# A two-block transformer kernel: weight split moved behind convolution and token sums on VectorE, and three projections back to eight block products

## The chip, the cores and the metric

The kernel runs on one core of one Trainium2 chip. The metric is the device time of one execution in microseconds; lower is better. The kernel before takes 2741.47 us (median of three runs, 2741.23 to 2741.66).

The engines are named as in the profile: PE is TensorE (PEld its weight loads), DVE is VectorE, ACT is ScalarE, POOL is GpSimd, SP is SyncE, which here issues the weight loads. All of them run their own instruction stream in order and wait for one another through semaphores.

## The reference

Two transformer blocks run one after the other on 512 tokens of width 1024, all in float32. Between them they hold five feed-forward networks (FFNs) with a hidden width of 2816, which take most of the time. The first has a short convolution on its gate, the other four are SwiGLU layers:

```
def conv_ffn(n, w_up, conv_w, conv_b, w_down):          # FFN 0
    u, g = jnp.split(n @ w_up, 2, axis=-1)
    gp = jnp.pad(g, ((0, 0), (pad, pad), (0, 0)))
    gc = sum(gp[:, j:j + S] * conv_w[j] for j in range(CONV_WIDTH)) + conv_b
    return (jax.nn.silu(gc) * u) @ w_down

def swiglu(x, w_gate, w_up, w_down):                    # FFNs 1 to 4
    return (jax.nn.silu(x @ w_gate) * (x @ w_up)) @ w_down
```

Each FFN reads an RMS-normalised input and adds its result to the residual stream. Around them stand a linear recurrence, windowed attention, cross attention to a memory, a pooling and latent-attention mixer and a gated convolution mixer. The change does not touch those.

## The kernel before, in words

**Numbers as pairs.** Every float32 operand of a product is held as two parts: `hi`, the value rounded to the type that TensorE multiplies, and `lo`, the rest. A product is three matmuls (lines 2023 to 2025): hi by hi, lo by hi, hi by lo. Weights arrive in chunks of 128 x 2048 values. SP loads a chunk into one of two `stage` buffers, ACT writes `w_hi` (line 525), DVE writes `w_lo = stage - w_hi` (line 1024, `split_lo`, called by `ffn_lo`), and PE waits for `w_lo` (semaphore `lo_ready`) before it begins the chunk. All three buffers exist twice, so the split of chunk p+2 can begin only when PE has finished chunk p.

**The order of an FFN.** `ORDER` lists the 30 chunks of an FFN: `gate 0, up 0, gate 1, up 1`, then `gate it, up it, down it-2` for `it` from 2 to 9, then `gate 10, up 10`. Four short chunks follow (the "tail", the last part of the down projection). I call a place in this list p: chunk 0 is gate 0, chunk 2 gate 1, chunk 4 gate 2, chunk 5 up 2, chunk 6 down 0, chunk 7 gate 3. A gate or an up chunk gives two tiles of 128 hidden columns by 512 tokens.

**Eight or seven products.** A gate or up chunk is a product of 2 x 2 blocks. The plain form (`eight`) does it with 48 matmuls of 512 columns. The other form (`seven_products`) is a Strassen scheme: seven block products, 84 matmuls of 256 columns. Which chunk takes which form is in the table `SEVENS`. The seven-product form needs sums of token blocks (`token_sums`, lines 1090 to 1095, once per FFN, rounded into `t_hi` by ACT and `t_lo` by DVE at line 1100), sums of weight blocks for every chunk (`weight_sums`, lines 1050 to 1055, four instructions, and `s_hi`, `s_lo` by line 1037), and five instructions instead of one to collect the result from PSUM (`evacuated`, lines 1075 to 1083). In FFN 0 the gates 3 to 10 and the ups 4, 6 and 8 use seven products, the other chunks eight. In FFNs 1 to 4 gates and ups use seven from `it` = 2 on.

**The order on DVE.** DVE does one step per chunk p, begun when PE has finished chunk p (line 1154): it evacuates the result from PSUM, makes the weight sums of chunk p+2 if that is a seven-product up, splits the weights of chunk p+2 (`ffn_lo`), then does in FFN 0 the convolution of a gate (`convolved`, six instructions, lines 1145 to 1149), then the token sums that are due at this p (`T_SUMS`: in FFN 0 half of them at p = 0 and half at p = 2, in the other FFNs all at p = 0), then `t_lo`, the weight sums of a gate at p+3, and `f_lo`, the lo part of the finished hidden tiles. At the start of an FFN a statistic over the tokens (line 2063 or 2068 on PE, a square root on ACT, a reciprocal on DVE, line 1104) has to be there before the first evacuation.

ACT applies the SiLU to the gate (line 603 in FFN 0, 606 in the others), POOL multiplies gate and up (line 1901), ACT rounds the product to `f_hi` (line 615), and down chunks read `f_hi` and `f_lo`.

Of the kernel before, what the change touches and what calls it, by code (L numbers as in the profile page):

```python
# [51 lines left out]
STEPS = FT // 2  # L52
# [13 lines left out]
TILES = {"gate": 2, "up": 2, "down": 4}  # L66
TILE_AT = [sum(TILES[kind] for kind, _ in ORDER[:p]) for p in range(len(ORDER) + 1)]
LAST_K = 4 * ((STEPS - 3) // 2)
SEVENS = [{"gate": range(3, STEPS), "up": range(4, STEPS - 1, 2)}] + 4 * [{"gate": range(2, STEPS), "up": range(2, STEPS - 1)}]


def _ffn(i):
# [59 lines left out]
def past(n):  # L132

    return n + 1


def free(ap, offset, dims):

    return bass.AP(tensor=ap.tensor, offset=ap.offset + offset, ap=[ap.ap[0]] + dims)


def build(nc, stream, x_in, mem_in, pos_in, par_in, const_in, out):
    ctx = ExitStack()
    with ctx:
# [154 lines left out]
        def sem(name):  # L299
            return ctx.enter_context(nc.semaphore(name))  # L300
# [24 lines left out]
        f_hi_ready, f_ready = sem("f_hi_ready"), sem("f_ready")  # L325
# [64 lines left out]
        SINGLES = 3 * KP * P  # L390
        SEVEN_ORDER = [(i, p) for i in range(5) for p, (kind, it) in enumerate(ORDER) if kind != "down" and it in SEVENS[i][kind]]
        NTH = {at: n for n, at in enumerate(SEVEN_ORDER)}
# [13 lines left out]
        def two_banks(p):  # L406

            return 6 if p % 2 == 0 else 0

        def four_banks(p):  # L410

            return 4 * (p % 2 == 0)
# [10 lines left out]
        T_SUMS = [{0: [0, 1], 2: [2, 3]}] + 4 * [{0: [0, 1, 2, 3]}]  # L423
# [588 lines left out]
        def _(dve):  # L1012
# [48 lines left out]
            def evacuated(i, p, to):  # L1061

                if (i, p) not in NTH:
                    b = two_banks(p)
                    dve.tensor_tensor(to, ps[:, b:b + 2, :], free(rstd[:, :], 0, [[0, 2], [1, S]]), ALU.mult).then_inc(acc_evac, 2)
                    return
                n, bank = NTH[i, p], four_banks(p)

                def product(which, dims):
                    b, half = PRODUCT[which]  # L1070
                    return free(ps[:, bank + b, :], HALF * half, dims)

                adjacent, twice_dims = [[HALF, 2], [1, HALF]], [[0, 2], [1, HALF]]
                dve.wait_ge(first_copied, n + 1)
                dve.tensor_tensor(blocks[:, 0:2, :], product(2, adjacent), free(first, 0, twice_dims), ALU.add).then_inc(blocks_sum, 1)
                dve.wait_ge(blocks_sum, 4 * n + 1)
                dve.tensor_tensor(blocks[:, 2, :], product(7, [[1, HALF]]), blocks[:, 1, :], ALU.add).then_inc(blocks_sum, 1)
                dve.wait_ge(blocks_sum, 4 * n + 2)
                dve.tensor_tensor(free(blocks[:, 1, :], 0, [[S, 2], [1, HALF]]), product(5, twice_dims), blocks[:, 1:3, :], ALU.add).then_inc(blocks_sum, 1)
                dve.wait_ge(blocks_sum, 4 * n + 3)  # L1080
                dve.tensor_tensor(blocks[:, 1:3, :], product(3, adjacent), blocks[:, 1:3, :], ALU.add).then_inc(blocks_sum, 1)
                dve.wait_ge(blocks_sum, 4 * n + 4)
                dve.tensor_tensor(to, free(blocks[:, 0, :], 0, [[S, 2], [1, S]]), free(rstd[:, :], 0, [[0, 2], [1, S]]), ALU.mult).then_inc(acc_evac, 2)  # L1083

            def token_sums(i, j):

                done, gain = 16 * i + 4 * j, (pc(GAIN[i], j), pc(GAIN[i], KP + j))
                b12, b21, b22 = h[:, j, HALF:S], h[:, KP + j, 0:HALF], h[:, KP + j, HALF:S]
                dve.wait_ge(t_scaled, 4 * i + j + 1)
                dve.scalar_tensor_tensor(t_f[:, T1, j, :], b12, gain[0], t_f[:, T3, j, :], ALU.mult, ALU.subtract).then_inc(t_sum, 1)  # L1090
                dve.wait_ge(t_sum, done + 1)
                dve.scalar_tensor_tensor(t_f[:, T2, j, :], b22, gain[1], t_f[:, T1, j, :], ALU.mult, ALU.subtract).then_inc(t_sum, 1)
                dve.wait_ge(t_sum, done + 2)
                dve.tensor_tensor(t_f[:, T3, j, :], t_f[:, T2, j, :], t_f[:, T3, j, :], ALU.subtract).then_inc(t_sum, 1)
                dve.scalar_tensor_tensor(t_f[:, T4, j, :], b21, gain[1], t_f[:, T2, j, :], ALU.mult, ALU.subtract).then_inc(t_sum, 1)
# [38 lines left out]
            def ffn(i):  # L1134

                scale = SCALE[f"down{i}"]

                def convolved(it):

                    for e in range(2):  # L1140
                        f = 2 * it + e
                        g = gate_b[:, e, :]
                        if e == 0:
                            dve.wait_ge(acc_evac, T0["up0"] + TILE_AT[ORDER.index(("gate", it))] + 2)
                        dve.tensor_scalar(up_b[:, e, :], g[:, 1:1 + S], pc("conv_w1", f), pc("conv_b", f), ALU.mult, ALU.add).then_inc(conv_step, 1)
                        dve.wait_ge(conv_step, 6 * it + 3 * e + 1)
                        dve.scalar_tensor_tensor(up_b[:, e, :], g[:, 0:S], pc("conv_w0", f), up_b[:, e, :], ALU.mult, ALU.add).then_inc(conv_step, 1)
                        dve.wait_ge(conv_step, 6 * it + 3 * e + 2)
                        dve.scalar_tensor_tensor(up_b[:, e, :], g[:, 2:2 + S], pc("conv_w2", f), up_b[:, e, :], ALU.mult, ALU.add).then_inc(conv_step, 1)

                for p, (kind, it) in enumerate(ORDER):
                    c, t = chunk_at(i, p)
                    f, k = FT * i + 2 * it, 2 * it % 8
                    dve.wait_ge(chunk_done, c + 1)
                    if kind == "down":
                        b, m = four_banks(p), 4 * (it % 2)
                        if i == 1 and it < 2:
                            dve.wait_ge(renormed, KT + m + 4)
                        dve.scalar_tensor_tensor(h[:, m:m + 4, :], ps[:, b:b + 4, :], scale, h[:, m:m + 4, :], ALU.mult, ALU.add).then_inc(acc_evac, 4)
                    elif kind == "gate":  # L1160
                        evacuated(i, p, gate_b[:, :, 1:1 + S])
                    elif it < STEPS - 1:
                        dve.wait_ge(f_ready, past(f))
                        if i == 0:
                            dve.wait_ge(silu_ready, f + 2)
                        evacuated(i, p, up_b[:, :, :])
                    else:
                        dve.wait_ge(f_ready, past(f))
                        for e in range(2):
                            if i == 0:  # L1170
                                dve.wait_ge(silu_ready, f + 2)
                            dve.tensor_tensor(up_b[:, e, :], ps[:, two_banks(p) + e, :], rstd[:, :], ALU.mult).then_inc(acc_evac, 1)
                        for e in range(2):
                            dve.wait_ge(f_hi_ready, f + e + 1)
                            dve.tensor_tensor(f_lo[:, k + e, :], up_b[:, e, :], f_hi[:, k + e, :].bitcast(F32), ALU.subtract).then_inc(f_ready, 1)
                    if kind_at(i, p + 2) == ("up", True):
                        weight_sums(i, p + 2)
                    ffn_lo(i, p + 2)
                    if kind == "gate" and i == 0:
                        dve.wait_ge(f_ready, past(f))  # L1180
                        convolved(it)
                    for j in T_SUMS[i].get(p, []):
                        token_sums(i, j)
                    if p == T_ROUND[i]:
                        token_lo(i, 0)
                        token_lo(i, 1)
                    if p == T_ROUND[i] + 1:
                        token_lo(i, 2)
                        token_lo(i, 3)
                    if kind_at(i, p + 3) == ("gate", True):  # L1190
                        weight_sums(i, p + 3)
                    if kind == "up" and it < STEPS - 1:
                        dve.wait_ge(f_hi_ready, f + 2)
                        dve.tensor_tensor(f_lo[:, k:k + 2, :], up_b[:, :, :], f_hi[:, k:k + 2, :].bitcast(F32), ALU.subtract).then_inc(f_ready, 2)
                    if i == 1 and (kind, it) == ("gate", 1):
                        dve.wait_ge(std_ready, NS0["renorm"] + 1)
                        dve.reciprocal(sq[:, :], ssum[:, :]).then_inc(rstd_ready, 1)
# [335 lines left out]
            for i, (j, side) in enumerate(BRANCHES):  # L1533
                gate = gates(j)
# [1371 lines left out]
```

## Time and profile before

| | |
|---|---|
| median of three runs | 2741.47 us |
| the profiled execution | 2741.47 us, of which its span is 2739.7 us |
| PE busy | 2708.2 us, 99% of the span |
| DVE busy | 2120.1 us, 77% |
| ACT busy | 1012.1 us, 37% |
| POOL busy | 594.2 us, 22% |
| TensorE clock granted, mean | 0.999 of full speed |
| DMA | 97 GB/s in the mean |

The span is the time from the first to the last instruction of the profiled execution, and 1.8 us lie around it. "Busy" counts the time in which an engine executes. Matmuls overlap in the pipeline, so the start of one to the start of the next says more than the duration of one. A row of the trace gives the start in us from the span's start, the duration in us, the engine, the line, the operation, the names written and read, the shape, and in square brackets how long the engine sat idle before it and what released it. `w_hi`, `w_lo` and `stage` stand without their buffer number.

### The profile page before, as it was taken

How to read it: one execution, taken by the hardware profiler on the slowest of the kernel's cores; microseconds unless marked ns; L12 is line 12 of the kernel's file. 1: busy time of each engine (PE TensorE's matmuls, PEld its weight loads, DVE VectorE, ACT ScalarE, POOL GpSimd, SP SyncE). 2: the span in 40 equal slices, each digit the busy share in tenths (PEclk: the TensorE clock that was granted, in tenths of full speed). 3: DMA queues.
4: the chain of work that ended last, by engine and by line, in shares of the span. 5: the costliest groups of instructions: out<-in, count | busy, mean ns of one | idle time of the engine just before them, and what ended most of it. 6: DMA issues, size and time to landing. Idle time of an engine off the chain costs nothing.

```text
span 2739.7 us, 38567 instructions
## 1 busy us (share of the span) xinstructions
PE 2708.2 (99%) x15680; PEld 2380.0 (87%) x15680; DVE 2120.1 (77%) x2088; ACT 1012.1 (37%) x1089; POOL 594.2 (22%) x314
## 2 busy tenths in 40 slices
PE   9999999999999999999999999999999999999999
PEld 7978889878888888999768899998999988889998
DVE  6778766558888789887576898978888765698884
ACT  4333524434333343333354433334333322243332
POOL 0124014041000382111322311114111142511110
PEclk9999999999999999999999999999999999999999
DMA  4212133222222322323311222232322332322322
GB/s 168 86 69 70 41 108 130 102 77 92 95 106 93 109 91 93 108 93 111 114 47 62 93 94 107 93 122 94 108 100 101 108 108 93 107 80 105 108 105 96
DMA packets 39760, 266.20 MB, mean 97 GB/s; under 512 B 4528, under 2 KB 5808, under 8 KB 8240
## 3 DMA queue, kind: packets, MB, share of 16 engines
q1 hardware_dynamic: 38016, 259.02, 26.9%
q10 hardware_dynamic: 1584, 4.87, 0.5%
q8 instruction: 123, 2.02, 0.3%
q14 instruction: 37, 0.30, 0.0%
HBM read 261.77 MB, written 2.10 MB: 96 GB/s over the span
## 4 chain that ended last, share of the span: by engine, by line
PE 91%; DVE 6%; issue 1%; ACT 1%; POOL 1%; DMA 0%; SPq 0%; DVEq 0%; POOLq 0%; ACTq 0%
PE ps L2023 28%; PE ps L2024 28%; PE ps L2025 28%; PE ps L2253 1%; DVE w_lo L1024 1%; PE ps L2319 1%; PE ps L2350 1%; PE ps L2641 1%; PE ps L2613 1%; PE ps L2275 1%; DVE s_lo L1037 0%; DVE t_lo L1100 0%; PE ps L2333 0%; ACT w_hi L525 0%; POOL sq L1872 0%
## 5 line engine op out<-in xcount | busy, mean ns | idle before, releaser
L525 ACT ACTIVATE w_hi<-stage 128x2048 fp32r<-128x2048 f32 (+1 forms) x241 | 418.5, 1737 | 601.0 <-PE ps L2025 598.6
L2023 PE MATMUL ps<-x_hi,w_hi 128*128 128x512 f32 (+1 forms) x1768 | 632.0, 357 | 0.8 <-DVE w_lo L1203 0.6
L2024 PE MATMUL ps<-x_lo,w_hi 128*128 128x512 f32 (+1 forms) x1768 | 621.8, 352 | 0.0
L2025 PE MATMUL ps<-x_hi,w_lo 128*128 128x512 f32 (+1 forms) x1768 | 621.7, 352 | 0.0
L1024 DVE TENSOR_TENSOR w_lo<-stage,w_hi 128x2048 fp32r<-128x2048 f32 (+1 forms) x241 | 571.5, 2371 | 42.5 <-ACT w_hi L525 42.5
L1901 POOL TENSOR_TENSOR up_b<-up_b,gate_b 128x1024 f32<-128x1024 f32 x50 | 182.0, 3640 | 1198.6 <-DVE up_b L1083 924.5
L2023 PEld LDWEIGHTS ps<-x_hi,w_hi 128*128 128x128 f32 x1768 | 335.1, 190 | 47.6 <-issue 3.6
L2024 PEld LDWEIGHTS ps<-x_lo,w_hi 128*128 128x128 f32 x1768 | 335.2, 190 | 45.8 <-issue 3.6
L2025 PEld LDWEIGHTS ps<-x_hi,w_lo 128*128 128x128 f32 x1768 | 334.8, 189 | 44.8
L2023 PE MATMUL ps<-f_hi,w_hi 128*128 128x512 f32 x880 | 343.2, 390 | 2.4 <-DVE w_lo L1024 2.4
L2024 PE MATMUL ps<-f_lo,w_hi 128*128 128x512 f32 x880 | 343.1, 390 | 0.0
L2025 PE MATMUL ps<-f_hi,w_lo 128*128 128x512 f32 x880 | 342.6, 389 | 0.0
L2023 PE MATMUL ps<-t_hi,s_hi 128*128 128x256 f32 x948 | 269.8, 285 | 11.1 <-DVE w_lo L1024 8.2
L542 ACT ACTIVATE s_hi<-s_f 128x2048 fp32r<-128x2048 f32 x79 | 151.6, 1919 | 335.0 <-PE ps L2025 295.3
L2025 PE MATMUL ps<-t_hi,s_lo 128*128 128x256 f32 x948 | 269.3, 284 | 0.0
L2024 PE MATMUL ps<-t_lo,s_hi 128*128 128x256 f32 x948 | 269.3, 284 | 0.0
L1037 DVE TENSOR_TENSOR s_lo<-s_f,s_hi 128x2048 fp32r<-128x2048 f32 x79 | 187.8, 2377 | 46.2 <-ACT s_hi L542 46.2
L2023 PEld LDWEIGHTS ps<-f_hi,w_hi 128*128 128x128 f32 x880 | 165.4, 188 | 36.1 <-DVE w_lo L1024 2.6
L2023 PEld LDWEIGHTS ps<-t_hi,s_hi 128*128 128x128 f32 x948 | 182.7, 193 | 15.7 <-DVE w_lo L1024 9.9
L2025 PEld LDWEIGHTS ps<-f_hi,w_lo 128*128 128x128 f32 x880 | 165.3, 188 | 34.5
L2024 PEld LDWEIGHTS ps<-f_lo,w_hi 128*128 128x128 f32 x880 | 165.4, 188 | 32.8
L2024 PEld LDWEIGHTS ps<-t_lo,s_hi 128*128 128x128 f32 x948 | 182.7, 193 | 1.4
(443 smaller groups left out, 4791.4 us busy)
## 6 DMA issues: line engine op xcount, KB each, us to landing
stage<-in_stream SPq DMA_DIRECT2D x242, 1024.0 KB, 4.9
h<-in_x ACTq DMA_DIRECT2D x2, 1024.0 KB, 5.5
out_x<-h SPq DMA_DIRECT2D x8, 256.0 KB, 2.1
h<-in_x SPq DMA_DIRECT2D x6, 256.0 KB, 3.8
mem_raw<-in_mem ACTq DMA_DIRECT2D x1, 1024.0 KB, 5.0
stage<-in_stream SPq DMA_DIRECT2D x6, 128.0 KB, 4.2
h<-in_x SPq DMA_DIRECT2D x1, 512.0 KB, 6.1
mask_f<-in_constants ACTq DMA_DIRECT2D x1, 448.0 KB, 6.1
```

Of the source, the lines that this page charges most:

```text
L525: act.activation(w_hi[slot][:, 0:width], stage[slot][:, 0:width], ACT.Copy).then_inc(hi_ready, 1)
L542: act.activation(s_hi[:, :], s_f[:, :], ACT.Copy).then_inc(s_rounded, 1)
L1024: dve.tensor_tensor(w_lo[slot][:, 0:width], stage[slot][:, 0:width], w_hi[slot][:, 0:width].bitcast(F32), ALU.subtract).then_inc(lo_ready, 1)
L1037: dve.tensor_tensor(s_lo[:, :], s_f[:, :], s_hi[:, :].bitcast(F32), ALU.subtract).then_inc(s_ready, 1)
L1901: pool.tensor_tensor(up_b[:, :, :], up_b[:, :, :], gate_b[:, :, 1:1 + S], ALU.mult).then_inc(prod_ready, 2)
L2023: pe.matmul(out_ap, wh, xh, start=first, stop=False)
L2024: pe.matmul(out_ap, wh, xl, start=False, stop=False)
L2025: return pe.matmul(out_ap, wl, xh, start=False, stop=last)
L2253: mm = pe.matmul(ps[:, bank, b * P:(b + 1) * P], lhs, rhs, start=True, stop=True)
L2275: mm = pe.matmul(ps[:, 5 + 2 * e, :], QQ[e][:, 0, b * P:(b + 1) * P], A[e][:, b, :], start=(b == 0), stop=(b == BLK - 1))
L2319: mm = pe.matmul(ps[:, bank, at:at + w], qa[:, j, n * P:(n + 1) * P], k_z[p][:, k0:k0 + w], start=(b < 2), stop=(n == 3))
L2350: mm = pe.matmul(ps[:, 6, n * P + WIN_D * p:n * P + WIN_D * (p + 1)], w_pT[p][:, at_bank, at:at + P], va[:, b, half], start=(b == WINDOW_O ...
```

## The change

Two things are changed in the FFNs. First, in the DVE step of a gate chunk the convolution (FFN 0) and the token sums (all FFNs) now come directly behind the evacuation, so ahead of the weight split of chunk p+2. Second, in FFN 0 no up chunk uses seven products any more: ups 4, 6 and 8 take the plain eight-product form, and their weight sums and five-part evacuations go.

```
-SEVENS = [{"gate": range(3, STEPS), "up": range(4, STEPS - 1, 2)}] + 4 * [...]
+SEVENS = [{"gate": range(3, STEPS), "up": range(0)}] + 4 * [...]
...
                     elif kind == "gate":
                         evacuated(i, p, gate_b[:, :, 1:1 + S])
+                        if i == 0:
+                            dve.wait_ge(f_ready, past(f))
+                            convolved(it)
+                        for j in T_SUMS[i].get(p, []):
+                            token_sums(i, j)
...
                     if kind_at(i, p + 2) == ("up", True):
                         weight_sums(i, p + 2)
                     ffn_lo(i, p + 2)
-                    if kind == "gate" and i == 0:
-                        dve.wait_ge(f_ready, past(f))
-                        convolved(it)
-                    for j in T_SUMS[i].get(p, []):
-                        token_sums(i, j)
                     if p == T_ROUND[i]:
```

On DVE, at the step of chunk 0 of FFN 2 (FFNs 1, 3 and 4 have the same two places), `w_lo` of chunk 2 leaves its place behind the evacuation:

```order
 L1104 RECIPROCAL rstd<-ssum 128x512
 L1065 TENSOR_TENSOR gate_b<-ps,rstd 128x2x512
-L1024 TENSOR_TENSOR w_lo_57<-stage_53,w_hi_55 128x2048
 L1090 SCALAR_TENSOR_TENSOR t_f<-h,par,t_f 128x256
 L1092 SCALAR_TENSOR_TENSOR t_f<-h,par,t_f 128x256
```

and stands again behind the last of the 16 token-sum instructions, ahead of the evacuation of chunk 1:

```order
 L1094 TENSOR_TENSOR t_f<-t_f 128x256
 L1095 SCALAR_TENSOR_TENSOR t_f<-h,par,t_f 128x256
+L1024 TENSOR_TENSOR w_lo_57<-stage_53,w_hi_55 128x2048
 L1065 TENSOR_TENSOR up_b<-ps,rstd 128x1024
 L1024 TENSOR_TENSOR w_lo_56<-stage_52,w_hi_54 128x2048
```

The two rows with a plus and a minus are the same instruction, 16 instructions later. In FFN 0 it moves past six convolution and eight token-sum instructions at chunk 0 and again at chunk 2.

On DVE in FFN 0, at the step of gate 3 (chunk 7), the kernel before has the weight split of the down chunk first and then the convolution:

```order
L1083 TENSOR_TENSOR gate_b<-blocks,rstd 128x2x512
L1024 TENSOR_TENSOR w_lo_56<-stage_52,w_hi_54 128x2048
L1145 TENSOR_SCALAR up_b<-gate_b,par 128x512
L1147 SCALAR_TENSOR_TENSOR up_b<-gate_b,par,up_b 128x512
L1149 SCALAR_TENSOR_TENSOR up_b<-gate_b,par,up_b 128x512
L1145 TENSOR_SCALAR up_b<-gate_b,par 128x512
L1147 SCALAR_TENSOR_TENSOR up_b<-gate_b,par,up_b 128x512
L1149 SCALAR_TENSOR_TENSOR up_b<-gate_b,par,up_b 128x512
L1050 TENSOR_TENSOR s_f<-stage_53 128x512
```

and the changed kernel has them the other way round:

```order
L1083 TENSOR_TENSOR gate_b<-blocks,rstd 128x2x512
L1145 TENSOR_SCALAR up_b<-gate_b,par 128x512
L1147 SCALAR_TENSOR_TENSOR up_b<-gate_b,par,up_b 128x512
L1149 SCALAR_TENSOR_TENSOR up_b<-gate_b,par,up_b 128x512
L1145 TENSOR_SCALAR up_b<-gate_b,par 128x512
L1147 SCALAR_TENSOR_TENSOR up_b<-gate_b,par,up_b 128x512
L1149 SCALAR_TENSOR_TENSOR up_b<-gate_b,par,up_b 128x512
L1024 TENSOR_TENSOR w_lo_56<-stage_52,w_hi_54 128x2048
L1050 TENSOR_TENSOR s_f<-stage_53 128x512
```

Here `w_lo_56` belongs to the down chunk two places on. The same exchange is made at the gates 3 to 9; behind gate 10 it is the first, shorter tail chunk.

## Rows read from the trace of the kernel before

**Rows 1.** All waits of PE for `w_lo`: total us, times, longest.

```profile
PE ps L2023 <- DVE w_lo L1024: 12.5, 7, 4.1
```

**Rows 2.** PE in FFN 0, timeline: start, us, what, [idle before].

```profile
691.74 0.40 PE L2023 MATMUL ps<-x_hi,w_hi 128*128 128x512 f32 x1
...
702.65 0.39 PE L2023 MATMUL ps<-f_hi,w_hi 128*128 128x512 f32 x1
...
723.60 0.28 PE L2023 MATMUL ps<-x_hi,w_hi 128*128 128x256 f32 x1
...
733.68 0.40 PE L2023 MATMUL ps<-f_hi,w_hi 128*128 128x512 f32 x1
...
744.36 0.39 PE L2025 MATMUL ps<-f_hi,w_lo 128*128 128x512 f32 x1
746.11 0.39 PE L2023 MATMUL ps<-t_hi,s_hi 128*128 128x256 f32 x1 [1.36 <-DVE w_lo L1024]
...
756.29 0.40 PE L2023 MATMUL ps<-x_hi,w_hi 128*128 128x512 f32 x1
```

**Rows 3.** DVE in FFN 0, the step of gate 3, timeline.

```profile
691.94 0.69 DVE L1075 TENSOR_TENSOR blocks<-ps,ssum 128x512 f32<-128x512 f32 x1 [5.51 <-PE ps L2025]
...
695.79 2.29 DVE L1024 TENSOR_TENSOR w_lo<-stage,w_hi 128x2048 fp32r<-128x2048 f32 x1
697.99 0.54 DVE L1145 TENSOR_SCALAR up_b<-gate_b,par 128x512 f32<-128x512 f32 x1
...
702.05 0.68 DVE L1050 TENSOR_TENSOR s_f<-stage 128x512 f32<-128x512 f32 x1
```

**Rows 4.** PE and DVE at the start of FFN 0, timeline.

```profile
616.61 0.40 PE L2024 MATMUL ps<-x_lo,w_hi 128*128 128x512 f32 x1
...
620.74 1.23 DVE L1065 TENSOR_TENSOR gate_b<-ps,rstd 128x1024 f32<-128x1024 f32 x1
...
624.08 0.54 DVE L1145 TENSOR_SCALAR up_b<-gate_b,par 128x512 f32<-128x512 f32 x1
...
628.15 0.48 DVE L1090 SCALAR_TENSOR_TENSOR t_f<-h,par,t_f 128x256 f32<-128x256 f32 x1
...
631.69 1.21 DVE L1065 TENSOR_TENSOR up_b<-ps,rstd 128x1024 f32<-128x1024 f32 x1
```

**Rows 5.** PE, DVE and ACT at the start of FFN 2, timeline.

```profile
1530.50 0.40 PE L2024 MATMUL ps<-x_lo,w_hi 128*128 128x512 f32 x1
...
1535.78 2.28 DVE L1024 TENSOR_TENSOR w_lo<-stage,w_hi 128x2048 fp32r<-128x2048 f32 x1
1537.98 0.48 DVE L1090 SCALAR_TENSOR_TENSOR t_f<-h,par,t_f 128x256 f32<-128x256 f32 x1
...
1541.43 1.92 ACT L525 ACTIVATE w_hi<-stage 128x2048 fp32r<-128x2048 f32 x1 [3.12 <-PE ps L2025]
...
1545.06 1.22 DVE L1065 TENSOR_TENSOR up_b<-ps,rstd 128x1024 f32<-128x1024 f32 x1
...
1562.70 0.39 PE L2025 MATMUL ps<-x_hi,w_lo 128*128 128x512 f32 x1
1563.75 0.36 PE L2023 MATMUL ps<-t_hi,s_hi 128*128 128x256 f32 x1 [0.67 <-DVE t_lo L1100]
```

**Rows 6.** PE in FFN 1, timeline.

```profile
1032.14 0.50 PE L2023 MATMUL ps<-f_hi,w_hi 128*128 128x512 f32 x1 [2.38 <-DVE w_lo L1024]
...
1047.49 0.39 PE L2023 MATMUL ps<-t_hi,s_hi 128*128 128x256 f32 x1 [4.13 <-DVE w_lo L1024]
...
1059.15 0.28 PE L2023 MATMUL ps<-x_hi,w_hi 128*128 128x256 f32 x1
```

**Rows 7.** Stretches: length, busy us of PE, PEld, DVE, ACT, POOL, then granted PEclk, DMA.

```profile
1032.10:1043.00 10.90, 10.86 (x48) 8.94 (x48) 10.66 (x10) 3.29 (x2) 5.46 (x4) 1.00 0.30 98
1047.40:1050.00 2.60, 2.51 (x15) 2.51 (x16) 2.60 (x3) 0.94 (x1) 0.00 (x0) 0.71 0.46 120
...
978.60:1057.00 78.40, 70.75 (x411) 62.35 (x410) 75.50 (x65) 32.48 (x26) 49.46 (x19) 0.98 0.24 83
```

More of the change, by code:

```diff
@@ L68 @@
 LAST_K = 4 * ((STEPS - 3) // 2)
-SEVENS = [{"gate": range(3, STEPS), "up": range(4, STEPS - 1, 2)}] + 4 * [{"gate": range(2, STEPS), "up": range(2, STEPS - 1)}]
+SEVENS = [{"gate": range(3, STEPS), "up": range(0)}] + 4 * [{"gate": range(2, STEPS), "up": range(2, STEPS - 1)}]
 def _ffn(i):
```

## The prediction

> **What bounds the kernel now.** The page's first part shows PE busy for 99% of the span; its chain of waits is PE for 91%. So the time is the sum of PE's chunks, and only what lengthens a chunk or makes PE wait counts. I read next the list of waits for PE's rows: in the whole kernel it waits for `w_lo` of line 1024 seven times, 12.5 us in total, 4.1 us at the longest [rows 1]. Then PE's timeline where those waits stand: three of them are in FFN 0, 1.4 us each, at the gate behind a seven-product up [rows 2], and three more in FFN 1 [rows 6]. Last I read DVE's timeline ahead of each chunk, because what releases PE is always one split instruction there. The question at each place is how far ahead of its use the `w_lo` was, and how much work the change puts in front of it.
>
> Three measures from rows are used throughout. An eight-product chunk takes 702.65 - 691.74 = 10.91 us, thus 0.227 us per 512-column matmul; a seven-product chunk takes 733.68 - 723.60 = 10.08 us [rows 2]. A chunk that PE had to wait for starts 0.06 us after its `w_lo` ends and then loses about 0.1 us in restarting (746.11 to 756.29 is 10.18 instead of 10.08 us) [rows 2]. On DVE, the next instruction starts about 0.08 us before the duration of the last is over, except behind one whose result it reads.
>
> **A. Three ups go back to eight products.** Each costs PE 10.91 - 10.08 = 0.83 us. In return DVE loses four weight sums, one `s_lo` and four small evacuations per up. The gate two chunks on was late for exactly this: 744.36 to 746.11 is 1.75 us where 0.23 is due, so 1.52 us, and 0.10 for the restart [rows 2]. The gates behind a plain up show no wait, so I take all of it as gone. Net -1.62 + 0.83 = -0.79, three times: **-2.4 us**. Bounds: the gain can't exceed this wait, and without it the edit costs +2.5.
>
> **B. The steady gates of FFN 0 (gates 3 to 9).** Now the convolution stands ahead of the down chunk's split. DVE starts at 691.94 and is done evacuating at 695.79; the convolution takes 702.05 - 697.99 = 4.06 us and, reading what was just written, starts 0.12 later than the split did; the split takes 2.28 [rows 3]. It ends at 695.79 + 0.12 + 4.06 + 2.28 = 702.25. PE wants it at 702.65 less one matmul (the weights of the next are loaded meanwhile) and the 0.06: 702.36 [rows 2]. So 0.1 us is left: **0 us**, hidden by the up chunk in between. If that cover is gone, the price is what it is late by, up to 0.3 us at each of seven gates, 2.1 us.
>
> **C. The start of FFN 0.** DVE's first evacuation starts at 620.74 and takes 1.23; it can't be earlier, it waits for the reciprocal. Now the convolution (628.15 - 624.08 = 4.07) and eight token sums (631.69 - 628.15 = 3.54) come before the split (2.28): 620.74 + 1.23 + 0.03 + 4.07 + 3.54 + 2.28 = 631.89, so PE starts chunk 2 at 631.95 [rows 4]. It is due at 616.61 + 47 x 0.227 = 627.28. Wait 4.67, restart 0.1. At chunk 2's end the same happens again with a punctual DVE: from 0.2 us after the first matmul of chunk 3 it needs 1.23 + 0.03 + 4.07 + 3.54 + 2.28 = 11.15 us, and 0.06, against 10.91: another 0.5 and 0.1. Sum **+5.4 us**. Behind DVE's late split nothing else is late: the evacuation of chunk 1 follows, whose bank PE needs only two chunks on.
>
> **D. The start of FFNs 2, 3 and 4.** Before, `w_lo` of chunk 2 runs at 1535.78, ahead of 16 token sums of 1545.06 - 1537.98 = 7.08 us. Now the sums come first: 1535.78 + 7.08 + 2.28 + 0.06 = 1545.20. Chunk 2 is due at 1530.50 + 47 x 0.227 = 1541.17; that chunk 1 is over by then shows in ACT, whose `w_hi` waits for it and starts at 1541.43 [rows 5]. Wait 4.03, restart 0.1. This takes the place of one wait that goes: chunk 4 waited for `t_lo`, 1563.75 - 1562.70 - 0.23 = 0.82 [rows 5], and DVE comes to `t_lo` at the old time while PE comes 4 us later. Net 3.3 us; the pattern stands three times (FFNs 2, 3, 4): **+9.9 us**. Also moved: SP's load of chunk 4 waits for this split and is issued 7.1 us later, at 1545.1. A load lands in 4.9 us (the page's part on DMA issues), so at 1550.0. Its first reader, the weight sums of chunk 4, stands in DVE's stream behind an evacuation, a split (together 3.4 us from 1545.1) and two `t_lo` instructions, so behind 1550 as well; I take the load as hidden.
>
> **E. The start of FFN 1.** The same 4 us wait arises, but here DVE is the slow engine: it is busy for 75.5 of the 78.4 us from 978.6 to 1057.0 [rows 7], and PE waits for it 2.38 and 4.13 us at chunks 6 and 7 [rows 6]. DVE's work is the same in another order, so the new wait is mostly paid out of these. It isn't all free: the renorm statistic is a PE instruction behind chunk 2, and ACT and DVE instructions that wait for it come up to 4 us later. I bound this term by -1.5 (the old 4.13 wait shrinks so far that its clock loss, see F, goes) and +3.3 (nothing more is absorbed than in D) and take **+0.5 us**.
>
> **F. The clock.** After the 4.13 us wait in FFN 1 the granted clock is 0.71 in the stretch from 1047.4 to 1050.0: more than half of it at 1.2 GHz instead of 2.4, after PE had idled. After the wait of 2.38 it is 1.00 [rows 7]. The chunk behind the long wait took 1059.15 - 1047.49 = 11.66 us instead of 10.08 [rows 6]; less the restart that is 1.5 us. The four new waits in FFNs 0, 2, 3 and 4 leave PE idle for about 4.5 and three times 3.9 us, between these two cases and much nearer the one with the loss. I count it for the first and for two of the other three: 3 x 1.5 = **+4.5 us**. Bounds 0 and 6.0.
>
> The Trainium skill speaks against the change here: "TensorE: Matmul & The Clock Gate", section "HAM oscillation — how this bites in real kernels", says that idle gaps of a few microseconds between groups of matmuls put the array back to half its clock, and that each such gap pays for the way back. By that rule all four waits lose, and the sum would be 1.5 us higher. The row at 1047.4 agrees with it; whether 3.9 us are enough no row of this trace shows.
>
> **Sum.** -2.4 + 0 + 5.4 + 9.9 + 0.5 + 4.5 = +17.9 us on a span of 2739.7, so 2757.6; with the 1.8 us around it 2759.4 us. The profiled execution took exactly the median of the runs, 2741.47, so nothing is to be corrected.
>
> **The rivals.**
>
> *R1, absorbed everywhere: 2739.1 us, not slower.* The place is chunks 4 to 7 of each FFN. If DVE rather than PE paces them, as in FFN 1, a PE that comes 4 us late to chunk 2 only waits less later on, and C to F vanish: -2.4 alone. It decides at the point where DVE's lag behind PE is over 4 us. For it: FFN 1. Against: in FFN 2 PE waits just 0.82 us in this stretch [rows 5] and in FFN 0 not at all before the three seven-product ups.
>
> *R2, the earlier sums pay: 2728 us.* The token sums end 2.2 us earlier, so `t_hi` and `t_lo` could; then the three 0.8 us waits, and in FFN 1 its waits of 2.4 and 4.1 and the clock loss of 1.5, would go: -2.4 - 2.8 - 8.0 = -13.2. It needs the split of chunk 2 to be free, that is `w_lo` at 1545.1 not to be wanted before; the due time of 1541.2 speaks against it, and `t_lo` still stands behind two splits and an evacuation in DVE's stream.
>
> *R3, the clock holds: 2755 us.* As forecast, without F. For it: one loss only in 2740 us, after the longest wait of all, and none after 2.38. Against: 3.9 and 4.5 are near 4.13.
>
> *R4, the thin margin of B breaks: 2761.5 us.* As forecast, and 0.3 us at each of seven gates. For it: a margin of 0.1 us. Against: the instructions on DVE repeat to 0.02 us.
>
> **How the numbers follow.** The forecast has a chance of 0.57, R3 0.20, R4 0.15, R1 0.05 and R2 0.03. What a measurement of this kernel can tell from no change is about 0.2%, 5.5 us. The forecast, R3 and R4 are all slower by more: 0.92. R1 is within it: 0.05. R2 is faster: 0.03. The range must take in R3 and R4 and the bounds of E and F: low, no clock loss and E at -1.5, 2753; high, all four losses and E half-way to its bound with B's price, 2741.5 + 17.9 + 1.5 + 1.4 + 2.1 = 2764.4. The range 2752 to 2765 leaves out R1, R2 and the outermost combinations, together over one in ten.
>
> **What would show it in the profile of the changed kernel.** PE's waits for `w_lo` should rise from 12.5 us to about 25: five waits of 3.7 to 4.6 us, one at chunk 2 of every FFN, the first ending at about 631.9, each released by line 1024. The three waits of 1.36 us at gates 5, 7 and 9 (A) should be gone, as the `t_lo` waits before chunk 4 of FFNs 2 to 4 (D). A granted clock below 1.00 in the 3 to 5 us behind the new waits shows F. At gates 3 to 9 PE should go from up to down without a gap (B). DVE should lose about 27 instructions. The forecast is wrong if `w_lo` of chunk 2 is released before PE has finished chunk 1, or if PE's waits later in FFNs 2 to 4 shrink by as much as the new one adds.

## The result, and the profile after

The changed kernel takes 2765.51 us (median of four runs, 2764.47 to 2766.23), the kernel before 2741.41 us beside it (2741.23 to 2741.66). The ratio is 1.0088, with a 95% interval of 1.007 to 1.0105: slower by 24.1 us. The forecast was 2759.4 us with a range that ended at 2765. The sign and the new waits came as forecast; one term, the clock, was counted at half its size. The profiled execution took 2763.61 us, span 2761.8, mean granted clock 0.995. Of all the runs in this document one was slow from end to end, 4507.58 us at a granted clock of 0.555, with the kernel that takes up 2 of FFN 1 to eight products (its five others took 2731.79 to 2732.25 us), and its ratio leaves that run out.

The waits of PE for `w_lo`, total us, times, longest, against [rows 1]:

```profile
PE ps L2023 <- DVE w_lo L1024: 25.8, 10, 4.6
```

12.5 became 25.8 us ("about 25" was written), and PE has no row for `t_lo` any more. PE itself is busy for 2720.1 us instead of 2708.2. Three ups with eight products account for 2.5 of these 11.9 us; the rest is the first sign that matmuls ran at a lower clock. Chunks 2 and 4 of FFN 0, PE's timeline (start, us, what, [idle before]), against the due times read from [rows 4]:

```profile
626.72 0.39 PE L2025 MATMUL ps<-x_hi,w_lo 128*128 128x512 f32 x1
631.71 0.79 PE L2023 MATMUL ps<-x_hi,w_hi 128*128 128x512 f32 x1 [4.60 <-DVE w_lo L1024]
632.30 0.63 PE L2024 MATMUL ps<-x_lo,w_hi 128*128 128x512 f32 x1
...
634.98 0.40 PE L2025 MATMUL ps<-x_hi,w_lo 128*128 128x512 f32 x1
...
654.71 0.39 PE L2025 MATMUL ps<-x_hi,w_lo 128*128 128x512 f32 x1
655.63 0.50 PE L2023 MATMUL ps<-x_hi,w_hi 128*128 128x512 f32 x1 [0.53 <-DVE w_lo L1024]
```

The figure in brackets counts from the end of the last matmul. The prediction reckons from start to start, less one matmul; so reckoned the waits are 631.71 - 626.72 - 0.23 = 4.76 and 655.63 - 654.71 - 0.23 = 0.69 us, where 4.67 and 0.5 were forecast. Behind the first, matmuls start 0.43 us apart instead of 0.23 until 634.4: that is the clock, not a wait. The steady gates, DVE at gate 3 and PE at the two places that answer to [rows 2] and [rows 3]:

```profile
698.67 0.69 DVE L1075 TENSOR_TENSOR blocks<-ps,ssum 128x512 f32<-128x512 f32 x1 [5.51 <-PE ps L2025]
...
702.71 0.55 DVE L1145 TENSOR_SCALAR up_b<-gate_b,par 128x512 f32<-128x512 f32 x1
...
706.78 2.29 DVE L1024 TENSOR_TENSOR w_lo<-stage,w_hi 128x2048 fp32r<-128x2048 f32 x1
```

```profile
709.15 0.39 PE L2025 MATMUL ps<-x_hi,w_lo 128*128 128x512 f32 x1
709.38 0.39 PE L2023 MATMUL ps<-f_hi,w_hi 128*128 128x512 f32 x1
...
752.12 0.28 PE L2023 MATMUL ps<-t_hi,s_hi 128*128 128x256 f32 x1
```

The split ends at 709.07. Taken back by one matmul and 0.06 us from the down chunk's start at 709.38, PE wanted it at 709.09: 0.02 us to spare, and no gap. At each of the gates 3 to 9 the split ends 0.30 or 0.31 us before the down chunk starts, and that start follows the last matmul by 0.23 us. At 752.12 stands the gate that used to wait 1.36 us; it now follows without one.

The start of FFN 2, DVE and then PE, against [rows 5]:

```profile
1540.13 1.23 DVE L1065 TENSOR_TENSOR gate_b<-ps,rstd 128x1024 f32<-128x1024 f32 x1
1541.27 0.47 DVE L1090 SCALAR_TENSOR_TENSOR t_f<-h,par,t_f 128x256 f32<-128x256 f32 x1
...
1548.36 2.28 DVE L1024 TENSOR_TENSOR w_lo<-stage,w_hi 128x2048 fp32r<-128x2048 f32 x1
```

```profile
1546.43 0.39 PE L2025 MATMUL ps<-x_hi,w_lo 128*128 128x512 f32 x1
1550.69 0.80 PE L2023 MATMUL ps<-x_hi,w_hi 128*128 128x512 f32 x1 [3.88 <-DVE w_lo L1024]
1551.29 0.63 PE L2024 MATMUL ps<-x_lo,w_hi 128*128 128x512 f32 x1
...
1555.56 0.63 PE L2025 MATMUL ps<-x_hi,w_lo 128*128 128x512 f32 x1
1555.98 0.50 PE L2023 MATMUL ps<-x_hi,w_hi 128*128 128x512 f32 x1
```

The sums take 7.09 us, the split follows them, and PE waits: 3.88 us in brackets, 1550.69 - 1546.43 - 0.23 = 4.03 us from start to start. Then twelve matmuls run slow. The clock in the stretches behind the five new waits (length, busy us of PE, PEld, DVE, ACT, POOL, then the granted PEclk, DMA), against [rows 7]:

```profile
631.70:635.20 3.50, 3.50 (x9) 2.79 (x10) 3.28 (x2) 0.00 (x0) 2.25 (x1) 0.59 0.63 218
993.50:997.00 3.50, 3.50 (x9) 2.79 (x10) 3.50 (x3) 1.94 (x3) 2.26 (x1) 0.58 0.66 218
1550.70:1556.00 5.30, 5.30 (x13) 4.14 (x14) 5.30 (x3) 1.99 (x4) 3.89 (x1) 0.50 0.73 226
1903.90:1907.60 3.70, 3.67 (x10) 2.85 (x11) 3.70 (x3) 1.95 (x3) 2.42 (x1) 0.56 0.69 213
2431.10:2436.50 5.40, 5.36 (x13) 4.19 (x14) 5.40 (x3) 2.09 (x4) 3.89 (x1) 0.50 0.75 228
```

In FFNs 2 and 4 the mean is 0.50 over 5.3 us and more, that is 1.2 GHz throughout; in the other three it is 0.56 to 0.59 over 3.5 to 3.7 us, so 1.2 GHz for most of the stretch and 2.4 GHz at its end. What a stretch costs is read from PE's timeline: the start of the 21st matmul behind the wait, less 20 x 0.227 us and the 0.1 of the restart. That gives 1.35, 1.4, 2.6, 1.6 and 2.7 us, together 9.65. A sixth loss, 1.5 us, stands in FFN 1 behind a later wait of 1.84 us.

From the first matmul behind one FFN's statistic to the next (FFN 1 from its statistic to the mixer behind it, FFN 4 to the end of the span), in us:

| | before | changed | difference | forecast, clock in it |
|---|---|---|---|---|
| FFN 0 | 357.35 | 361.94 | +4.6 | +4.5 |
| FFN 1 | 357.68 | 358.88 | +1.2 | +0.5 |
| FFN 2 | 347.39 | 353.24 | +5.85 | FFNs 2 to 4 |
| FFN 3 | 347.39 | 352.26 | +4.9 | together |
| FFN 4 and end | 340.1 | 346.0 | +5.9 | +12.9 |

The sum is 22.4, less 0.3 by which FFN 0 began earlier: the 22.1 us between the spans. The stretches between the FFNs agree within 0.02 us.

### The profile page after: what moved, and what is told of

It reads as the page before. It is cut to its first block, busy times and chain, and to the rows that moved or that the text cites. A ratio compares the mean times of both kernels' runs of the same rounds, so it can differ in the third digit from the quotient of the medians.

```text
span 2761.8 us, 38306 instructions
## 1 busy us (share of the span) xinstructions
PE 2720.1 (98%) x15572; PEld 2382.9 (86%) x15572; DVE 2100.4 (76%) x2061; ACT 1006.1 (36%) x1083; POOL 580.6 (21%) x314
## 4 chain that ended last, share of the span: by engine, by line
PE 92%; DVE 5%; ACT 1%; issue 1%; POOL 1%; DMA 0%; SPq 0%; DVEq 0%; POOLq 0%; ACTq 0%
PE ps L2023 29%; PE ps L2025 28%; PE ps L2024 28%; DVE w_lo L1024 1%; PE ps L2253 1%; PE ps L2319 1%; PE ps L2350 1%; PE ps L2641 1%; PE ps L2613 1%; PE ps L2275 1%; DVE rstd L1104 0%; DVE t_f L1092 0%; PE ps L2333 0%; ACT w_hi L525 0%; POOL sq L1872 0%
## 5 line engine op out<-in xcount | busy, mean ns | idle before, releaser
L2023 PE MATMUL ps<-x_hi,w_hi 128*128 128x512 f32 (+1 forms) x1792 | 648.5, 362 | 22.9 <-DVE w_lo L1024 22.4
L525 ACT ACTIVATE w_hi<-stage 128x2048 fp32r<-128x2048 f32 (+1 forms) x241 | 419.8, 1742 | 636.7 <-PE ps L2025 634.4
L2025 PE MATMUL ps<-x_hi,w_lo 128*128 128x512 f32 (+1 forms) x1792 | 637.3, 356 | 0.0
L2024 PE MATMUL ps<-x_lo,w_hi 128*128 128x512 f32 (+1 forms) x1792 | 637.3, 356 | 0.0
L1901 POOL TENSOR_TENSOR up_b<-up_b,gate_b 128x1024 f32<-128x1024 f32 x50 | 170.7, 3415 | 1234.8 <-DVE up_b L1083 830.4
L2024 PEld LDWEIGHTS ps<-x_lo,w_hi 128*128 128x128 f32 x1792 | 342.5, 191 | 48.4 <-issue 3.6
L2023 PE MATMUL ps<-t_hi,s_hi 128*128 128x256 f32 x912 | 258.0, 283 | 0.9 <-DVE w_lo L1024 0.9
L2025 PE MATMUL ps<-t_hi,s_lo 128*128 128x256 f32 x912 | 258.1, 283 | 0.0
L2024 PE MATMUL ps<-t_lo,s_hi 128*128 128x256 f32 x912 | 258.1, 283 | 0.0
L2023 PEld LDWEIGHTS ps<-t_hi,s_hi 128*128 128x128 f32 x912 | 174.9, 192 | 3.0 <-DVE w_lo L1024 1.3
L2024 PEld LDWEIGHTS ps<-t_lo,s_hi 128*128 128x128 f32 x912 | 174.9, 192 | 1.7
```

The costliest lines, as they stand in the source:

```text
L525: act.activation(w_hi[slot][:, 0:width], stage[slot][:, 0:width], ACT.Copy).then_inc(hi_ready, 1)
L1901: pool.tensor_tensor(up_b[:, :, :], up_b[:, :, :], gate_b[:, :, 1:1 + S], ALU.mult).then_inc(prod_ready, 2)
L2023: pe.matmul(out_ap, wh, xh, start=first, stop=False)
L2024: pe.matmul(out_ap, wh, xl, start=False, stop=False)
L2025: return pe.matmul(out_ap, wl, xh, start=False, stop=last)
```

## The experiments

Theory 1 is that of the prediction: late splits make PE wait once per FFN, and the idle PE then loses its clock. Its rivals are named with each run. "Before" is the median of the kernel before on the same chip.

**The ups alone.** The kernel before with the change's table:

```
-SEVENS = [{"gate": range(3, STEPS), "up": range(4, STEPS - 1, 2)}] + 4 * [...]
+SEVENS = [{"gate": range(3, STEPS), "up": range(0)}] + 4 * [...]
```

> The kernel before with one part of the change alone: in FFN 0 no up chunk uses seven products, the order on DVE stays the old one. Theory (term A: each up costs PE 0.83 us more and removes a wait of 1.62 us at the gate behind it): 2741.4 - 2.4 = 2739.0 us, PE's three waits of 1.36 us in FFN 0 gone. Rival (the wait had another cause than the up's extra DVE work, so it stays): 2741.4 + 2.5 = 2743.9 us, the waits still there.

Measured: 2737.69 us against 2740.37, ratio 0.9991 (0.9982 to 1.0), so -2.7 us, with a total wait of PE for `w_lo` of 6.8 us in four places. Term A (-2.4) holds: this half of the change is a small gain. In the trace FFN 0 takes 354.89 us against 357.35, -2.45 us, and PE's three waits of 1.36 us are gone. FFN 1 is shorter too, 356.15 us against 357.68, though nothing is changed in it. What differs is where the clock fell: before, behind the last long wait (4.13 us); here, behind the one ahead of it, for eight slow matmuls or 1.6 us.

```profile
1029.66 0.56 PE L2023 MATMUL ps<-f_hi,w_hi 128*128 128x512 f32 x1 [2.37 <-DVE w_lo L1024]
...
1044.96 0.39 PE L2023 MATMUL ps<-t_hi,s_hi 128*128 128x256 f32 x1 [2.55 <-DVE w_lo L1024]
```

PE then came 1.6 us later to the next wait, which shrank from 4.13 to 2.55 us: a loss of clock ahead of a wait for DVE costs nothing here, one behind the last such wait costs its 1.5 us.

**The order alone.** The changed kernel with the old table.

> The changed kernel with ups 4, 6 and 8 of FFN 0 on seven products again: the new order on DVE alone. Theory (the whole loss comes from the order, and the two parts add up): 2765.5 + 2.4 = 2767.9 us, and up to 2 us more since w_lo of the down chunk is wanted 0.8 us earlier behind a seven-product up and comes late there. Rival (the two parts depend on each other, the order being harmless as long as the ups keep seven products): well under 2760 us.

Measured: 2768.2 us, ratio 1.0102 (1.0087 to 1.0118), +27.8. The two halves add up within the noise: -2.7 + 27.8 = 25.1 against the 24.1 of both. The trace has, as the expectation allowed for, three new waits of 0.41 us at the down chunks behind the seven-product ups. The whole loss is in the order on DVE.

**PE kept busy while it waits.** In the changed kernel PE does spare matmuls before chunk 2 of each FFN, into the bank that the chunk then clears:

```
+FILL = [19, 16, 16, 16, 16]
...
+                if p == 2:
+                    pe.wait_ge(acc_evac, T0[f"up{i}"] + TILE_AT[p - 1])
+                    for j in range(FILL[i]):
+                        pe.matmul(ps[:, two_banks(p), :], x_hi[:, 0, 0:P], x_hi[:, 0, :], start=True, stop=True)
                 clear(i, p)
```

> The changed kernel, but at chunk 2 of each FFN PE first runs 16 matmuls of 512 columns (19 in FFN 0) into the PSUM bank that chunk 2 overwrites anyway, so that it is busy during most of the wait for w_lo; no result uses them and no instruction of another engine is moved. Theory (beyond the waits themselves the loss is the clock: granted clock 0.50 for 3.4 to 6.8 us behind each wait): the matmuls cost nothing, the clock stays at 1.00 behind them, and the time is what terms A to E give, 2741.4 - 2.4 + 5.4 + 9.9 + 0.5 = 2754.8 us. Rival (the slow stretch has nothing to do with PE idling, or DVE and ACT set the pace behind chunk 2): 2765 us as before, or more if the added matmuls are in the way.

Measured: 2755.24 us, ratio 1.0054 (1.004 to 1.0068), +14.9. PE at FFN 2, and then the clock behind the start of chunk 2 in FFN 0 and in FFN 2 (lines are one or more higher in this kernel):

```profile
1544.12 3.79 PE L2102 MATMUL ps<-x_hi 128*128 128x512 f32 x16
1548.17 0.50 PE L2024 MATMUL ps<-x_hi,w_hi 128*128 128x512 f32 x1 [0.26 <-DVE w_lo L1025]
```

```profile
631.80:635.30 3.50, 3.45 (x15) 2.83 (x16) 3.33 (x2) 0.00 (x0) 2.20 (x1) 1.00 0.64 199
1548.10:1553.50 5.40, 5.33 (x23) 4.42 (x24) 5.40 (x4) 2.10 (x4) 3.89 (x1) 1.00 0.77 225
```

The split comes no earlier, PE still can't start chunk 2, and yet 9.2 us of the 24.1 are gone, because the clock stays at 1.00 (2.4 GHz). DVE and DMA have the same load in these stretches, so it was not they that slowed the matmuls. This is the measure of term F: 9.2 us by the medians, with some 6 us of doubt from the intervals of the two ratios. The traces are sharper. With the waits filled the FFNs take 360.68, 357.47, 350.69, 350.68 and 343.34 us, which is 1.3, 1.4, 2.5, 1.6 and 2.7 us less than in the changed kernel, 9.5 in all: one by one the losses read from PE's timeline (9.65). Against before they are +3.3, -0.2, +3.3, +3.3 and +3.3 us, the price of the waits with the clock held.

**Half as many spare matmuls**: `FILL = 5 * [8]`.

> As the run with filled waits (2755.2 us), but with only 8 matmuls of 512 columns (1.8 us) at chunk 2 of each FFN, so that PE is idle for about 2.1 us there instead of 3.9 (2.7 us in FFN 0). Theory 1 (a loss of the clock needs the whole wait of some 3.9 us; a wait of 2.38 us left it at 1.00 in the kernel before): 2755 us, clock at 1.00 behind these waits. Theory 2 (what my term F left out: shorter idle time can lose the clock too, and whether it does depends on when it falls; the changed kernel shows a stretch at half clock behind a wait of 1.84 us in FFN 1): up to 1.5 us for each of five waits, 2757 to 2763 us.

Measured: 2756.81 us against 2740.27, ratio 1.0062 (1.0048 to 1.0077), +16.5, between the two theories: the four runs took 2755.72, 2756.24, 2757.38 and 2760.87 us. In the trace (2756.24 us) only the shortened wait of FFN 1 is followed by a loss. PE's first matmul behind three of the shortened waits, and the next:

```profile
631.71 0.50 PE L2024 MATMUL ps<-x_hi,w_hi 128*128 128x512 f32 x1 [2.78 <-DVE w_lo L1025]
632.04 0.39 PE L2025 MATMUL ps<-x_lo,w_hi 128*128 128x512 f32 x1
...
992.13 0.72 PE L2024 MATMUL ps<-x_hi,w_hi 128*128 128x512 f32 x1 [2.03 <-DVE w_lo L1025]
992.65 0.63 PE L2025 MATMUL ps<-x_lo,w_hi 128*128 128x512 f32 x1
...
1550.06 0.50 PE L2024 MATMUL ps<-x_hi,w_hi 128*128 128x512 f32 x1 [2.06 <-DVE w_lo L1025]
1550.39 0.40 PE L2025 MATMUL ps<-x_lo,w_hi 128*128 128x512 f32 x1
```

A wait of 2.03 us was followed by the loss, one of 2.78 and three of 2.06 were not. The length of the wait alone does not decide.

**The convolution alone in front.** The changed kernel with the token sums back behind the split:

```
                             convolved(it)
-                        for j in T_SUMS[i].get(p, []):
-                            token_sums(i, j)
...
                     ffn_lo(i, p + 2)
+                    for j in T_SUMS[i].get(p, []):
+                        token_sums(i, j)
```

> The changed kernel with the token sums back behind the weight split in all FFNs; the convolution of FFN 0 still stands ahead of the split and the ups still use eight products. Theory: in FFNs 1 to 4 nothing is left of the change; in FFN 0 the split of chunk 2 ends at 620.74 + 1.26 + 4.07 + 2.28 = 628.35 in the old trace's time, 1.1 us late, chunk 4 is in time, and the steady gates keep their margin of 0.1 us: 2741.4 - 2.4 + 1.2 = 2740.2 us. Rival (the margin of 0.1 us at gates 3 to 9 does not hold, 0.3 us each): 2742.3 us, with small waits of PE for w_lo at the down chunks.

Measured: 2738.9 us, ratio 0.9994 (0.9985 to 1.0003), -1.5 against before. PE at chunk 2 of FFN 0:

```profile
628.63 0.50 PE L2023 MATMUL ps<-x_hi,w_hi 128*128 128x512 f32 x1 [1.06 <-DVE w_lo L1024]
```

Moving the convolution costs that one wait; against the run with the ups alone it is +1.2 us. At gates 3 to 9 PE has no gap, so B's margin holds here too. The price of the change is in the token sums.

**The token sums in front in FFN 1 only**, on top of the last kernel (`if i == 1:` ahead of the first loop, `i != 1` on the second).

> The run with the convolution alone moved (2738.9 us), with the token sums ahead of the split in FFN 1 only. It measures term E. Theory (DVE paces the start of FFN 1, so the new wait at chunk 2 is paid out of the waits at chunks 5, 6 and 7): 2738.9 + 1.2 = 2740.1 us, the 1.2 from comparing the two traces over FFN 1. Rival (the wait adds as in FFNs 2 to 4, 4.9 to 5.9 us each in the traces): 2744 to 2745 us.

Measured: 2741.88 us against 2740.27, ratio 1.0006 (0.9998 to 1.0015). That is 3.1 us more than the kernel it builds on, though each of the two differences is uncertain by some 2.4 us; in the two traces FFN 1 takes 359.09 us against the 357.38 us of the kernel it builds on, 1.7 more. That 357.38 holds a loss of 1.25 us behind the last long wait of FFN 1, and its profiled execution (2740.27 us) lies 1.4 above its median. Against the 356.15 us of the ups alone, which has the same order in FFN 1 and no such loss at the end, the difference is 2.9 us. PE in FFN 1:

```profile
988.09 0.80 PE L2026 MATMUL ps<-x_hi,w_hi 128*128 128x512 f32 x1 [3.85 <-DVE w_lo L1024]
988.69 0.63 PE L2027 MATMUL ps<-x_lo,w_hi 128*128 128x512 f32 x1
...
1024.51 0.39 PE L2026 MATMUL ps<-x_hi,w_hi 128*128 128x256 f32 x1 [1.84 <-DVE w_lo L1024]
```

The 3.85 us are mostly paid back, as term E has it (the rival had 5 to 6 us): of the 2.9 us they leave 1.3. The clock loss behind them, 1.6 us, is not. The one behind 1.84 us is: the wait after it is 0.88 us here, and 2.38 us in the second trace of the changed kernel, below, where no clock was lost behind the wait at chunk 5.

**The change once more**, as a second look at where the slow matmuls fall.

> The changed kernel itself once more, on the same chip and in the same rounds as the run beside it, for a firmer figure to set the others against. Theory: ratio to the kernel before 1.009 as in its first runs, with a spread of about 2 us from where the clock losses fall; rival (the first runs were an accident of one chip): below 1.007.

Measured: 2765.41 us against 2741.47, ratio 1.0087 (1.0073 to 1.01). The clock behind the waits in FFNs 0 and 1, a later one in FFN 1, and those in FFNs 2, 3 and 4:

```profile
631.70:638.30 6.60, 6.01 (x14) 4.75 (x15) 3.87 (x3) 0.78 (x1) 3.88 (x1) 0.50 0.68 220
...
995.60:999.10 3.50, 3.47 (x11) 2.76 (x12) 3.50 (x3) 1.99 (x3) 2.22 (x1) 0.69 0.65 211
1032.50:1036.00 3.50, 3.47 (x29) 3.48 (x30) 3.50 (x2) 2.18 (x3) 3.42 (x2) 1.00 0.66 206
1553.50:1557.00 3.50, 3.46 (x9) 2.73 (x10) 3.50 (x3) 1.96 (x3) 2.21 (x1) 0.54 0.65 204
1905.60:1911.00 5.40, 5.34 (x13) 4.18 (x14) 5.40 (x4) 2.09 (x4) 3.89 (x1) 0.50 0.72 221
2434.00:2438.00 4.00, 3.93 (x11) 3.12 (x12) 4.00 (x4) 1.98 (x3) 2.68 (x1) 0.58 0.74 227
```

The same five waits lose again, but the long losses are now in FFN 0 and FFN 3, where they were in FFNs 2 and 4. By the same reading as before they cost 2.9, 1.7, 1.5, 2.8 and 1.6 us, 10.5 in all. The trace of the order alone is a third draw: again all five, the long ones in FFNs 2 and 4. Nothing in these traces tells where a long loss falls; two of five are long in each of the three.

**Towards a faster kernel.** The next three build on the ups alone, whose PE waits for DVE are nearly all in FFN 1. First, up 2 of FFN 1 is taken from seven products to eight, which relieves DVE there: `{"gate": range(2, STEPS), "up": range(3, STEPS - 1)}` for FFN 1.

> The run with only the ups of FFN 0 changed (2737.7 us, old order on DVE), and in FFN 1 up 2 (chunk 5) takes eight products too. Theory (PE's waits at chunks 6 and 7 of FFN 1, 2.38 and 4.13 us, and the half clock behind the second come from DVE's work; four weight sums, an s_lo and four evacuations less take about 9 us off it ahead of chunk 7, for 0.83 us more on PE): 2737.7 - 2.4 - 4.1 - 1.5 - 0.5 + 0.8 = 2730.0 us. Rival (POOL's renorm work or ACT holds these chunks up, not the amount of DVE's work): 2738.5 us.

Measured: 2732.03 us against 2740.27, ratio 0.9968 (0.9955 to 0.9981), -8.2; 2.0 us short of the expectation. A wait of 1.19 us stays at chunk 7 of FFN 1; and the expectation took off 4.13 us and a clock loss of 1.5 behind it, where the trace of the ups alone has 2.55 us and a loss that this wait had already paid for. Second, the `f_lo` of up 0 goes one step later in FFNs 1 to 4, to bring `t_lo` forward:

```
+                        if i and p == 2:
+                            dve.wait_ge(prod_ready, FT * i + 2)
                         evacuated(i, p, gate_b[:, :, 1:1 + S])
...
-                    if kind == "up" and it < STEPS - 1:
+                    late = i and p == 2
+                    if (kind == "up" and it < STEPS - 1 and not (i and p == 1)) or late:
```

> As the run before in this list, and in FFNs 1 to 4 the f_lo of up 0 moves on DVE from the end of step 1 to behind the last two t_lo in step 2, so that t_lo of the token sums is done 1.2 us earlier (the evacuation of gate 1 waits for POOL's product instead). Theory (chunk 4 of FFNs 2 to 4 waits 0.82 us and loses 0.1 in restarting, only for DVE's t_lo): another 2.7 us less, 2727.3 us. Rival (ACT's t_hi or the evacuation is late next, so nothing comes earlier): 2730 us.

Measured: 2732.07 us against 2740.27, ratio 0.9967 (0.9954 to 0.998): no gain. DVE in step 2 of FFN 2 shows why:

```profile
1548.38 2.29 DVE L1037 TENSOR_TENSOR s_lo<-s_f,s_hi 128x2048 fp32r<-128x2048 f32 x1 [0.85 <-ACT s_hi L542]
1550.59 1.75 DVE L1024 TENSOR_TENSOR w_lo<-stage,w_hi 128x1536 fp32r<-128x1536 f32 x1
1552.26 2.35 DVE L1100 TENSOR_TENSOR t_lo<-t_f,t_hi 128x1024 fp32r<-128x1024 f32 x2
```

DVE, rid of the `f_lo`, stands 0.85 us for ACT's `s_hi`, with `t_lo`, which is ready to go, queued behind. Third, therefore, the last two `t_lo` go ahead of `ffn_lo` in that step:

```
+                    if i and p == 2:
+                        token_lo(i, 2)
+                        token_lo(i, 3)
                     ffn_lo(i, p + 2)
```

> As the run with f_lo of up 0 moved (2732.1 us, no gain, because s_lo then waited 0.85 us for ACT's s_hi), and in step 2 of FFNs 1 to 4 the last two t_lo now come ahead of s_lo and w_lo of chunk 4, so that they fill this wait. Theory: all three are done 0.8 us earlier, at about the time at which PE can begin chunk 4, and the 0.9 us there goes in FFNs 2, 3 and 4: 2732.1 - 2.7 = 2729.4 us. Rival (another instruction of DVE or ACT is late in its place): 2732 us.

Measured: 2728.15 us (2728.08 to 2729.07) against 2741.47, ratio 0.9952 (0.9939 to 0.9966), -13.3: faster than both kernels of this case. Not all of the step from -8.2 to -13.3 is the edit: the median of the kernel before lies 1.2 us higher beside this run, though its runs cover nearly the same range (2739.87 to 2742.0 us, 2739.53 to 2741.87 beside the last). Against the last kernel it is 3.9 us by the medians. In the traces FFNs 2 to 4 give 0.7 us each and FFN 1 1.35. The same place on DVE, and PE's waits for `w_lo`:

```profile
1545.63 2.35 DVE L1100 TENSOR_TENSOR t_lo<-t_f,t_hi 128x1024 fp32r<-128x1024 f32 x2
1547.90 2.29 DVE L1037 TENSOR_TENSOR s_lo<-s_f,s_hi 128x2048 fp32r<-128x2048 f32 x1
1550.11 1.75 DVE L1024 TENSOR_TENSOR w_lo<-stage,w_hi 128x1536 fp32r<-128x1536 f32 x1
```

```profile
PE ps L2030 <- DVE w_lo L1024: 2.9, 2, 1.6
```

The `t_lo` fill the time in which `s_hi` is made, the splits behind them don't wait any more, and PE waits for `t_lo` nowhere.

## Why the prediction was right, and where it was not

**A** was right: -2.45 us in FFN 0 by the trace (-2.4 forecast), -2.7 by the medians, and the waits of 1.36 us are gone.

**B** was right at 0. The margin was 0.02 us and not 0.1, but DVE's and PE's instructions repeat so closely that even this held at all seven gates; rival R4 is out.

**C** was right: 4.76 and 0.69 us for 4.67 and 0.5. With the two restarts, A and the 1.35 us of clock that makes 4.55 of the 4.6 us of FFN 0.

**D** was right: the wait is the 4.03 us of the forecast (3.88 in brackets) at each of FFNs 2 to 4, 3.3 us net in each with the clock held, the `t_lo` waits before chunk 4 gone, SP's later load without a wait of its own. With the clock 5.9, 4.9 and 6.0 us against 5.85, 4.9 and 5.9 measured.

**E** was right in kind. With the clock held behind the new wait FFN 1 takes 357.47 us against 357.68, -0.2 us for +0.5 forecast: 1.3 us of the new wait are left over, and the old clock loss of 1.5 us behind the wait of 4.13 goes. What E and F both left out is the new loss behind the 3.85 us, 1.4 us, which no later wait pays for and which makes FFN 1 +1.2 us in the changed kernel. The loss behind the 1.84 us is paid for by the wait that follows. R1, that FFNs 0 and 2 to 4 absorb their waits as well, is out: in FFNs 2 to 4 no later wait but that of D was there to shrink, and the 14.9 us that remain with the clock held are far from its -2.4. R2 is out too: the earlier sums bring nothing that PE was waiting for.

**F is the step that failed**, by its size. The prediction put it: "I count it for the first and for two of the other three: 3 x 1.5 = +4.5 us. Bounds 0 and 6.0." Two things were wrong. All waits lost, in both traces of the changed kernel, that of FFN 1 included, which F did not count. And 1.5 us is not what a loss costs but the lesser of two sizes: the one row of before showed a short one, and two of five were about twice as long (2.6 and 2.7 us), so that the upper bound of 6.0 was none. In its place stand 9.2 us by the run that fills the waits, 9.65 us by the trace, 4.7 to 5.2 us above the forecast. On the profiled execution of the changed kernel the account closes: the losses of FFNs 0 and 2 to 4 are 8.25 us for 4.5, FFN 1 is 0.7 above its term, FFN 0 began 0.3 us earlier, and 2763.61 us is 4.2 above 2759.4. The median is 1.9 us higher still. The second trace, of an execution of 2765.41 us, has losses of 10.5 us, FFN 1 at +1.9 us and a start of FFN 0 that is 0.6 us later than in the first. R3, that the clock holds, is the kernel with the filled waits: 2755.24 us, for which it had 2755.

The rule of the Trainium skill, "TensorE: Matmul & The Clock Gate", section "HAM oscillation — how this bites in real kernels", that idle gaps of a few microseconds cost a way back at half the clock each time, was the better guide here than the single row: all ten waits of 3.8 to 4.6 us in the two traces of the changed kernel agree, and the five of the order alone. For waits of about 2 us, shorter than the gaps that the section speaks of, the runs show both outcomes.

## What to carry to other kernels

Where one engine makes the operand that the bound engine waits for, put that operand ahead of everything whose reader comes later; and where the maker itself has to wait, put ready work there, which gained 3.9 us here. Price a new wait of the matrix engine at its length plus the time at half clock behind it (1.4 to 2.9 us each here, for waits of 3.8 us and more). Where the engine soon waits again for the same maker, as in FFN 1, the later waits paid for most of the new one and for a loss just ahead of them, but not for the loss behind the first. Take a cost seen only once in a trace as one draw and not as a bound.

## What the runs showed of the hardware that was not expected

- The clock falls behind shorter waits than before's trace let expect. Eight slow matmuls of PE behind a wait of 2.35 us of the convolution kernel, FFN 1, where before had 1.00 behind 2.38 us:

```profile
1031.17 0.50 PE L2023 MATMUL ps<-f_hi,w_hi 128*128 128x512 f32 x1 [2.35 <-DVE w_lo L1024]
...
1032.20 0.56 PE L2024 MATMUL ps<-f_lo,w_hi 128*128 128x512 f32 x1
1032.57 0.63 PE L2025 MATMUL ps<-f_hi,w_lo 128*128 128x512 f32 x1
...
1035.55 0.46 PE L2023 MATMUL ps<-f_hi,w_hi 128*128 128x512 f32 x1
```

  Here the first four matmuls still ran 0.23 us apart, and only then the clock fell. Over all traces, losses stand behind waits of 1.81, 1.84, 2.03, 2.33, 2.35, 2.36, 2.37 and 2.52 us, none behind 2.06, 2.24, 2.38, 2.55 and 2.78, and none behind the waits for `w_lo` of 1.36 us and less. What decides between them stays open.
- A loss has two sizes, 5 to 8 or 11 to 13 matmuls of 512 columns at 0.43 us, and where the long ones fall differs between two runs of one kernel. Together with where a loss falls, ahead of a wait that pays for it or behind the last one, this is enough to explain that the runs of a kernel with waits scatter by some 1.6 us (2737.3 to 2737.9 and 2738.9 to 2739.4 with the ups alone). Two traces agree: that of the ups alone, from the lower group (2737.52 us), has no loss behind the last wait of FFN 1, and that of the convolution kernel, from the upper of its own groups (2740.27 us), has one of 1.25 us. It was not shown run by run.
